# Two score blocks behind each other in differential attention, value products moved behind scores in dilated attention

## Chip, cores and metric

The kernel runs on one core of one Trainium2 chip. The metric is the time of the program in device microseconds. TensorE (PE) does the matrix products, VectorE (DVE) and ScalarE (ACT) read PSUM and work elementwise, GpSimd (POOL) issues some transfers and sums some squares, SyncE (SP) issues the transfers of the weights. A bank is one of the eight PSUM banks of 128 x 512 float32.

## The reference, cut to what matters

The model has two blocks in a row: one layer of gated deltanet with retention and a gated MLP, and then two layers, of which the first mixes with dilated window attention and the second with differential attention, each with an MLP behind it. What is changed lies in the two attention layers of the second block.

```python
def differential_attention(xn, w_qkv, lam, subln_g, w_o, rel_bias, lambda_init):
    q = q.reshape(B, S, B_HEADS, 2, HEAD_DIM_2) * (HEAD_DIM_2 ** -0.5)     # 8 heads, 2 halves of 64
    ...
        logits = jnp.einsum('bqhjd,bkhjd->bhjqk', q_blk, k) + bias[None]
        p = jax.nn.softmax(logits, axis=-1)
        a = p[:, :, 0] - lam_full * p[:, :, 1]
        return jnp.einsum('bhqk,bkhe->bqhe', a, v)
    ...
    o = rms_norm(o, subln_g) * (1.0 - lambda_init)
    return o.reshape(B, S, B_HEADS * 2 * HEAD_DIM_2) @ w_o
```

The sequence has 512 tokens and is cut into 4 blocks of 128 queries; with 8 heads there are 32 blocks of scores, each for two halves j of 64 dimensions against 512 keys. Dilated window attention (16 heads of 64) is softmax(q k + bias) v over windows of keys, in three groups of heads.

## The kernel before

**Layers A and B.** Dilated attention is layer A, differential attention layer B. Each has a projection to queries, keys and values in 12 units of weights; a unit takes 16 steps on PE, a step is one tile and one slice of the contraction: three products of 128 x 128 weights with 512 columns (hi·hi, lo·hi, hi·lo of operands split in two, lines 901 to 903), or for units of values in layer B six of 256 columns (L1413 to L1415). So each layer has 192 steps, numbered 0 to 191. While PE makes the projection it also does the attention of the heads that are there already: tables written out by hand say behind which step each piece comes.

**One block of differential attention.** `block_scores` (L1522) multiplies half j of the queries with half j of the keys: both stand in 64 rows of the array, j = 0 in the upper, j = 1 in the lower, and go to two banks. Three passes (round·round, round·rest, rest·round) make six instructions for a block n. DVE's `scores(n)` (L2932, L2935) reads both banks, adds the bias and takes the maximum. ACT's `exps(n)` (L2306) makes the exponentials, DVE's `difference(n)` (L2942 to L2945) the difference of the two softmaxes. PE turns it with four transposes, `block_turned(n)` (helper at L1005), ACT's `block_taken(n)` (L2315) reads them. `head_values` (L1540) multiplies with the values in four chunks per head, ACT's `head_out` reads the sum, `head_lengths_b` (`brms`, L1499, L1500) sums the squares, `root` (L2249) reads these. `values_kept(u, bank)` (L2279) on ACT reads the two banks of a unit of values.

**Tables.** On PE: B_SCORES, B_TURNED, B_VALUES, B_SUMS. On DVE: B_SCORED (`scores`), B_DIFFS (`difference`), B_REST, B_LOW, B_SPLIT_LO. On ACT: B_EXPS, B_TAKEN, B_OUT, B_ROOTS, B_KEPT, B_SPLIT_HI. A key is a step, its value what is done there. On DVE and ACT the steps only give an order: each engine goes through its own list as fast as its waits let it. After step 191 a tail without a table does blocks 30 and 31 and begins the output projection (`output_b`).

**Banks.** PE asks for a bank with `ring_group`, which waits until the last user of that bank has been read; `BANKS` says which banks a piece may use, and `ring` lists all pieces in PE's order. Projection units use banks 0 and 1, the second unit of a layer banks 2 and 3. All score blocks of layer B use banks 4 and 5, the turned blocks bank 6, the value sums bank 7, `brms` banks 2 and 3.

**Layer A.** A pair of heads n has its scores (L1348, 16 instructions in two row halves, banks 4 and 5), its exponentials, its shares turned (`shares_turned`, 8 transposes, banks 6 and 7) and its value products (`weighted_values`, L1401, 16 instructions of 128 rows and 64 columns, bank 2). ACT's `head_pair` (table A_SUMMED) reads the value products. Within a step PE does scores, then turns, then value products.

Of the kernel before, what the change touches and what calls it, by code (L numbers as in the profile page):

```python
# [203 lines left out]
def build(nc, t, out):  # L204
# [15 lines left out]
    with ctx:  # L220
# [201 lines left out]
        def a_last(n):  # L422
# [11 lines left out]
        A_VALUES = {58: 0, 68: 1, 82: 2, 86: 3, 109: 4, 122: 5, 123: 6, 185: 7, 189: 8}  # L434
# [26 lines left out]
        B_DIFFS = {41: 0, 47: 1, 50: 2, 59: 3, 64: 4, 67: 5, 73: 6, 81: 7, 86: 8, 94: 9, 97: 10, 102: 11, 110: 12, 115: 13,  # L461
                    120: 14, 129: 15, 137: 16, 140: 17, 148: 18, 150: 19, 157: 20, 161: 21, 162: 22, 166: 23, 171: 24, 176: 25,
                    177: 26, 189: 27}
        B_TURNED = {48: 0, 51: 1, 62: 2, 65: 3, 70: 4, 72: 5, 81: 6, 85: 7, 96: 8, 98: 9, 103: 10, 108: 11, 113: 12, 120: 13,
                    125: 14, 132: 15, 139: 16, 145: 17, 152: 18, 154: 19, 163: 20, 167: 21, 169: 22, 179: 23, 186: 24, 189: 25,
                    190: 26}
        B_SCORES = {33: 0, 40: 1, 46: 2, 51: 3, 58: 4, 62: 5, 66: 6, 72: 7, 83: 8, 86: 9, 92: 10, 98: 11, 102: 12, 105: 13,
                    113: 14, 117: 15, 130: 16, 134: 17, 138: 18, 140: 19, 144: 20, 151: 21, 154: 22, 161: 23, 165: 24, 172: 25,
                    177: 26, 180: 27, 188: 28, 189: 29}
        B_VALUES = {67: (0, (0,)), 70: (0, (1,)), 71: (0, (2,)), 73: (0, (3,)), 88: (1, (0,)), 89: (1, (1,)), 90: (1, (2,)),  # L470
                    93: (1, (3,)), 112: (2, (0,)), 117: (2, (1,)), 118: (2, (2,)), 119: (2, (3,)), 133: (3, (0,)),
                    134: (3, (1,)), 136: (3, (2,)), 137: (3, (3,)), 181: (4, (0, 1)), 184: (4, (2, 3)), 188: (5, (0, 1)),
                    189: (5, (2, 3))}
        B_SUMS = {103: 0, 104: 1, 145: 2, 159: 3}
        B_ROOTS = {98: 0, 115: 1, 142: 2, 158: 3}
        B_SCALED = {110: (0,), 129: (1,), 160: (2,), 175: (3,)}
        B_HIGH = {167: (0, 1), 187: (2, 3)}
        B_LOW = {185: (0, 1), 190: (2, 3)}
        B_SCORED = {34: 0, 44: 1, 47: 2, 48: 3, 56: 4, 61: 5, 67: 6, 78: 7, 83: 8, 91: 9, 92: 10, 98: 11, 101: 12, 105: 13,
                    113: 14, 114: 15, 132: 16, 135: 17, 139: 18, 142: 19, 143: 20, 151: 21, 155: 22, 160: 23, 163: 24, 169: 25,  # L480
                    175: 26, 181: 27, 189: 28, 190: 29}
        B_EXPS = {38: 0, 41: 1, 44: 2, 49: 3, 56: 4, 61: 5, 66: 6, 78: 7, 81: 8, 86: 9, 91: 10, 97: 11, 99: 12, 108: 13,
                    112: 14, 120: 15, 131: 16, 132: 17, 136: 18, 145: 19, 150: 20, 153: 21, 159: 22, 161: 23, 166: 24, 169: 25,
                    172: 26, 183: 27, 189: 28, 190: 29}
        B_TAKEN = {42: 0, 51: 1, 57: 2, 59: 3, 66: 4, 69: 5, 80: 6, 83: 7, 89: 8, 95: 9, 103: 10, 107: 11, 114: 12, 121: 13,
                    126: 14, 130: 15, 140: 16, 148: 17, 152: 18, 159: 19, 161: 20, 164: 21, 168: 22, 174: 23, 186: 24, 189: 25,
                    191: 26}
        B_OUT = {72: 0, 88: 1, 123: 2, 133: 3, 175: 4, 191: 5}
        B_SPLIT_HI = {22: 1, 27: 2, 41: 3, 57: 4, 79: 5, 94: 6, 111: 7, 124: 8, 140: 9, 159: 10, 174: 11}
        B_SPLIT_LO = {26: 1, 39: 2, 52: 3, 70: 4, 91: 5, 100: 6, 125: 7, 132: 8, 153: 9, 167: 10, 187: 11}  # L490
        B_ROUND = {17: 0, 23: 1, 25: 2, 38: 3, 54: 4, 64: 5, 71: 6, 79: 7, 105: 8, 115: 9, 123: 10, 131: 11, 139: 12, 148: 13,
                    155: 14, 169: 15}
        B_REST = {21: 0, 27: 1, 28: 2, 39: 3, 62: 4, 71: 5, 75: 6, 82: 7, 107: 8, 116: 9, 123: 10, 133: 11, 143: 12, 156: 13,
                    158: 14, 177: 15}
# [6 lines left out]
        B_KEPT = {40: (2, 0), 47: (2, 1), 88: (5, 0), 95: (5, 1), 167: (10, 0), 173: (10, 1), 183: (11, 0)}  # L501
# [31 lines left out]
        for step in range(A_STEPS):  # L533
            ring += [("s", A_SCORES[step], e) for e in range(2)] if step in A_SCORES else []
            ring += [("pt", A_TURNED[step], e) for e in range(2)] if step in A_TURNED else []
            ring += [("pv", a_last(A_VALUES[step]))] if step in A_VALUES and a_last(A_VALUES[step]) is not None else []
# [7 lines left out]
        for step in range(B_STEPS):  # L544
            ring += [("bs", B_SCORES[step], j) for j in range(2)] if step in B_SCORES else []
            ring += [("at", B_TURNED[step])] if step in B_TURNED else []
            ring += [("bo", B_VALUES[step][0])] if step in B_VALUES and B_VALUES[step][1][-1] == TOK - 1 else []
            ring += [("brms", B_SUMS[step])] if step in B_SUMS else []
        ring += [("at", 27), ("bs", 30, 0), ("bs", 30, 1), ("at", 28), ("bs", 31, 0)]
        ring += [("bs", 31, 1), ("bo", 6), ("at", 29), ("brms", 4), ("brms", 5), ("at", 30), ("at", 31), ("bo", 7)]  # L550
        ring += [("brms", 6), ("brms", 7)]
# [5 lines left out]
                 "bs": (4, 5), "at": (6,), "bo": (7,), ("bo", 7): (5,),  # L557
                 "brms": (2, 3), ("norm", 7): (0,)}
        BANKS.update({("brms", h): (4, 5, 7) for h in range(4, DIFF_HEADS)})
        BANKS.update({("y", 4 * half + c): ((4, 5, 6, 7), (1, 2, 3, 4))[half][c:c + 1] for half in range(2) for c in range(TOK)})  # L560
        BANKS.update({name: tuple(range(8)) for name in MIXER_RING})
# [772 lines left out]
        def attention_a_parts(pe, step):  # L1334

            if step in A_SCORES:
                n = A_SCORES[step]
                tile = A_PAIRS[n][0]
                u, second = A_KEYS[n]
                if second:  # L1340
                    pe.wait_ge(bank_free, p_qkvs[0].g0 + u + 3)
                else:
                    pe.wait_ge(at("a_tile0"), u + 1)
                b = [ring_group(pe, ("s", n, e)) for e in range(2)]
                for k, (i, c) in enumerate(a_parts(n)):
                    for e, (group, _) in enumerate(a_heads(n)):
                        rows = slice(64 * e, 64 * e + 64)
                        ins = nc.tensor.matmul(b[e][:, k * P:(k + 1) * P], a_q[rows, tile, i * P:(i + 1) * P],  # L1348
                                               keys(a_k[rows, tile, :], group, c), start=True, stop=True)
                        if k == TOK - 1:  # L1350
                            ring_filled(ins)
            if step in A_TURNED:
                shares_turned(pe, A_TURNED[step])
            if step in A_VALUES:
                weighted_values(pe, A_VALUES[step])
# [61 lines left out]
        def layer_b_tensor(pe):  # L1417
# [95 lines left out]
        def block_scores(pe, n):  # L1513

            h, i = divmod(n, 4)
            if i == 0:
                pe.wait_ge(at("b_rest"), B_TILES.index((B_KEYS[h], h % 2)) + 1)
            b = [ring_group(pe, ("bs", n, j)) for j in range(2)]
            for k, (q_of, k_of) in enumerate(((b_round, b_round), (b_round, b_rest), (b_rest, b_round))):
                for j in range(2):  # L1520
                    rows = slice(64 * j, 64 * j + 64)
                    ins = nc.tensor.matmul(b[j][:, :], q_of(0, h)[rows, i * P:(i + 1) * P], k_of(1, h)[rows, :],  # L1522
                                           start=k == 0, stop=k == 2)
                    if k == 2:
                        ring_filled(ins)
# [714 lines left out]
        def layer_b_scalar(act):  # L2240
# [628 lines left out]
        def layer_b_vector(dve):  # L2869
# [238 lines left out]
```

## Time and profile before

| | |
|---|---|
| times, three runs | 1914.03, 1914.14, 1915.45 us (median 1914.14) |
| the profiled execution | 1912.97 us, of which the span shown is 1911.1 us |
| granted TensorE clock | 0.999 |
| PE busy | 1897.7 us (99%) |
| DVE, ACT, POOL busy | 1051.3, 808.4, 103.6 us |
| layer A's projection with attention | about 690 to 890 us of the span |
| layer B's projection with attention | about 1289 to 1512 us of the span |

The times of the profile are those of one execution. In the timeline each row is one instruction or several of one line merged (x6): its start, its length, and in a bracket the idle time before it and who ended it. Matrix products are pipelined, so each lasts longer (0.39 us) than the distance to the next start (0.23 us); what a piece costs PE is read from starts, not from lengths.

### The profile page before, as it was taken

How to read it: one execution, taken by the hardware profiler on the slowest of the kernel's cores; microseconds unless marked ns; L12 is line 12 of the kernel's file. 1: busy time of each engine (PE TensorE's matmuls, PEld its weight loads, DVE VectorE, ACT ScalarE, POOL GpSimd, SP SyncE). 2: the span in 40 equal slices, each digit the busy share in tenths (PEclk: the TensorE clock that was granted, in tenths of full speed). 3: DMA queues.
4: the chain of work that ended last, by engine and by line, in shares of the span. 5: the costliest groups of instructions: out<-in, count | busy, mean ns of one | idle time of the engine just before them, and what ended most of it. 6: DMA issues, size and time to landing. Idle time of an engine off the chain costs nothing.

```text
span 1911.1 us, 25491 instructions
## 1 busy us (share of the span) xinstructions
PE 1897.7 (99%) x9523; PEld 1510.6 (79%) x9523; DVE 1051.3 (55%) x1460; ACT 808.4 (42%) x1027; POOL 103.6 (5%) x90
## 2 busy tenths in 40 slices
PE   9999999999999999999999999999999999999998
PEld 7788878888888877777888888887767788888887
DVE  8657765776257667466442244337678644324423
ACT  6382464554134344444432133236666643213312
POOL 0010111000000040000100000010110010000001
PEclk9999999999999999999999999999999999999999
DMA  6223112322322253222223222333322222332231
GB/s 237 88 88 130 33 64 66 110 88 83 113 91 82 80 145 101 68 67 88 89 88 108 90 88 91 107 112 103 105 83 87 67 88 88 102 96 88 88 106 48
DMA packets 146483, 178.91 MB, mean 94 GB/s; under 512 B 3549, under 2 KB 140381, under 8 KB 143968
## 3 DMA queue, kind: packets, MB, share of 16 engines
q1 hardware_dynamic: 143008, 160.44, 25.9%
q0 software_dynamic: 3104, 17.10, 2.8%
q8 instruction: 53, 0.87, 0.2%
q10 hardware_dynamic: 288, 0.26, 0.0%
q14 instruction: 30, 0.25, 0.0%
HBM read 173.48 MB, written 2.20 MB: 92 GB/s over the span
## 4 chain that ended last, share of the span: by engine, by line
PE 96%; DVE 2%; ACT 1%; issue 0%; DMA 0%; SPq 0%; POOL 0%; DVEq 0%; ACTq 0%; POOLq 0%
PE bank L903 28%; PE bank L901 28%; PE bank L902 28%; PE bank L1005 2%; PE bank L1540 2%; PE bank L1522 1%; PE bank L1011 1%; PE bank L1413 1%; PE bank L1415 1%; PE bank L1414 1%; PE bank L1348 1%; PE bank L1401 1%; PE bank L1064 0%; PE bank L1099 0%; DVE w_lo L1631 0%
## 5 line engine op out<-in xcount | busy, mean ns | idle before, releaser
L1625 ACT ACTIVATE w_hi<-raw 128x2048 fp32r<-128x2048 f32 (+2 forms) x151 | 284.0, 1881 | 761.4 <-PE bank L903 756.1
L901 PE MATMUL bank<-n_hi,w_hi 128*128 128x512 f32 x1440 | 577.4, 401 | 2.1 <-DVE w_lo L1631 1.3
L903 PE MATMUL bank<-n_hi,w_lo 128*128 128x512 f32 x1440 | 571.9, 397 | 0.0
L902 PE MATMUL bank<-n_lo,w_hi 128*128 128x512 f32 x1440 | 568.9, 395 | 0.0
L1631 DVE TENSOR_TENSOR w_lo<-raw,w_hi 128x2048 fp32r<-128x2048 f32 (+2 forms) x151 | 340.1, 2252 | 276.6 <-ACT w_hi L1625 275.0
L902 PE MATMUL bank<-ff_lo,w_hi 128*128 128x512 f32 x848 | 334.3, 394 | 0.0
L901 PEld LDWEIGHTS bank<-n_hi,w_hi 128*128 128x128 f32 x1440 | 270.5, 188 | 75.2 <-issue 9.6
L902 PEld LDWEIGHTS bank<-n_lo,w_hi 128*128 128x128 f32 x1440 | 270.7, 188 | 67.5 <-issue 2.9
L903 PEld LDWEIGHTS bank<-n_hi,w_lo 128*128 128x128 f32 x1440 | 270.4, 188 | 63.2
L903 PE MATMUL bank<-ff_hi,w_lo 128*128 128x512 f32 x784 | 312.5, 399 | 0.0
L901 PE MATMUL bank<-ff_hi,w_hi 128*128 128x512 f32 x784 | 307.8, 393 | 0.0
L902 PEld LDWEIGHTS bank<-ff_lo,w_hi 128*128 128x128 f32 x848 | 159.2, 188 | 41.2 <-issue 0.5
L901 PEld LDWEIGHTS bank<-ff_hi,w_hi 128*128 128x128 f32 x784 | 147.1, 188 | 35.5 <-issue 0.3
L903 PEld LDWEIGHTS bank<-ff_hi,w_lo 128*128 128x128 f32 x784 | 147.2, 188 | 34.0
L2687 DVE SCALAR_TENSOR_TENSOR scratch<-bank,rstd 128x512 f32<-128x512 f32 x64 | 44.3, 692 | 149.9 <-PE bank L903 135.6
L2672 DVE TENSOR_TENSOR hT<-hT,bank 128x512 f32<-128x512 f32 (+1 forms) x70 | 48.1, 687 | 135.1 <-PE bank L903 132.2
L2438 DVE SCALAR_TENSOR_TENSOR scratch<-scratch,ffn_w 128x511 f32<-128x511 f32 x88 | 66.1, 751 | 16.8 <-DVE scratch L2438 6.0
L825 POOL TENSOR_TENSOR scratch<-scratch 128x1024 f32<-128x1024 f32 x5 | 13.5, 2709 | 960.5 <-ACT scratch L1756 960.5
L2932 DVE CUSTOM_DVE_ANT_0 scratch<-bank,b_bias 128x512 f32<-128x512 f32 x64 | 44.3, 692 | 28.2 <-PE bank L1522 25.6
L2306 ACT ACTIVATE scratch<-scratch,b_small 128x512 f32<-128x512 f32 x64 | 46.4, 724 | 21.5 <-DVE b_small L2935 19.9
L2426 DVE TENSOR_TENSOR scratch<-bank,rstd 128x512 f32<-128x512 f32 x44 | 30.4, 692 | 32.9 <-PE bank L903 23.2
L2694 DVE TENSOR_TENSOR ff_lo<-scratch,ff_hi 128x1024 f32 x32 | 39.2, 1226 | 8.1 <-ACT ff_hi L2162 7.9
(381 smaller groups left out, 1784.3 us busy)
## 6 DMA issues: line engine op xcount, KB each, us to landing
raw<-in_mlp_w_in SPq DMA_DIRECT2D x32, 1024.0 KB, 5.4
raw<-in_mlp_w_out SPq DMA_DIRECT2D x32, 1024.0 KB, 5.1
raw<-in_w_up SPq DMA_DIRECT2D x22, 1024.0 KB, 5.1
raw<-in_w_units SPq DMA_DIRECT2D x14, 1024.0 KB, 4.8
raw<-in_a_w_qkv SPq DMA_DIRECT2D x12, 1024.0 KB, 5.1
raw<-in_b_w_qkv SPq DMA_DIRECT2D x12, 1024.0 KB, 5.2
b_bias<-bias_table POOLq DMA_DIRECT2D x16, 448.0 KB, 4.4
raw<-in_w_down SPq DMA_DIRECT2D x8, 768.0 KB, 4.5
```

Source lines behind the costliest of these rows:

```text
L901: nc.tensor.matmul(b[:, :], w_hi[:, j % 2, cols], hi, start=start, stop=False)
L902: nc.tensor.matmul(b[:, :], w_hi[:, j % 2, cols], lo, start=False, stop=False)
L903: return nc.tensor.matmul(b[:, :], w_lo[:, j % 2, cols], hi, start=False, stop=final)
L1005: ins = nc.tensor.transpose(b[:, i * P:(i + 1) * P], src(i), ident)
L1625: act.activation(w_hi[:, s, cols], raw[:, s, cols], ACT.Copy).then_inc(hi_ready, 1)
L1631: dve.tensor_tensor(w_lo[:, s, cols], raw[:, s, cols], w_hi[:, s, cols].bitcast(F32), ALU.subtract).then_inc(lo_ready, 1)
L2306: done(act, act.activation(e, e, ACT.Exp, bias=b_small[:, 8 + 2 * (n % 4) + j:9 + 2 * (n % 4) + j], accum_out=b_small[:, 16 + 2 * (n % 4) ...
L2438: ins = dve.scalar_tensor_tensor(y, taken[:, n, 0:SEQ - back], w, y, ALU.mult, ALU.add)
L2672: ins = dve.tensor_tensor(h, h, b[:, :].unsqueeze(1), ALU.add)
L2687: ins = dve.scalar_tensor_tensor(scratch[:, 2 * g + tile, :], b[:, :], 0.0, rstd[:, :], ALU.max, ALU.mult)
L2694: done(dve, dve.tensor_tensor(ff_lo[:, bass.ds(it * 4 + 2 * g, 2), :], scratch[:, 2 * g:2 * g + 2, :], ff_hi[:, bass.ds(it * 4 + 2 * g, 2) ...
L2932: ring_done(dve, dve.tensor_tensor_reduce(b_s[:, n % 4, j, :], b[:, :], reversed_row(b_bias[:, h % 2, j, i * P:i * P + SEQ]), 1.0, -FAR, A ...
```

## The change

In layer B the scores of two blocks, 2m and 2m + 1, are made behind each other (`pair_scores(m)`, table B_PAIRS in place of B_SCORES): block 2m in banks 4 and 5, block 2m + 1 in banks 2 and 3 (the other way round for the last pair). `brms` stays in banks 2 and 3, which it now shares. All tables of layer B are laid out anew, mostly by a few steps; B_SUMS and B_ROOTS move by up to six. The tail does blocks 30 and 31 as one pair in front of the output products. In layer A value products come right behind scores where a step has both (`weighted_values` in front of `shares_turned`), and five of the value products change their step so that six of them share a step with scores (two before). A_SUMMED is not changed.

```diff
-        A_VALUES = {58: 0, 68: 1, 82: 2, 86: 3, 109: 4, 122: 5, 123: 6, 185: 7, 189: 8}
+        A_VALUES = {58: 0, 75: 1, 80: 2, 88: 3, 109: 4, 123: 5, 130: 6, 185: 7, 189: 8}
...
+        B_PAIRS = {37: 0, 47: 1, 58: 2, 67: 3, 82: 4, 91: 5, 102: 6, 113: 7, 130: 8, 137: 9, 143: 10, 152: 11, 167: 12, 176: 13,
+                    187: 14}
...
-        B_SCORES = {33: 0, 40: 1, 46: 2, 51: 3, 58: 4, 62: 5, 66: 6, 72: 7, 83: 8, 86: 9, 92: 10, 98: 11, 102: 12, 105: 13,
-                    113: 14, 117: 15, 130: 16, 134: 17, 138: 18, 140: 19, 144: 20, 151: 21, 154: 22, 161: 23, 165: 24, 172: 25,
-                    177: 26, 180: 27, 188: 28, 189: 29}
...
-        B_SUMS = {103: 0, 104: 1, 145: 2, 159: 3}
-        B_ROOTS = {98: 0, 115: 1, 142: 2, 158: 3}
+        B_SUMS = {108: 0, 111: 1, 150: 2, 165: 3}
+        B_ROOTS = {103: 0, 109: 1, 150: 2, 164: 3}
...
-            ring += [("bs", B_SCORES[step], j) for j in range(2)] if step in B_SCORES else []
+            ring += [("bs", 2 * B_PAIRS[step] + i, j) for i in range(2) for j in range(2)] if step in B_PAIRS else []
...
-                 "bs": (4, 5), "at": (6,), "bo": (7,), ("bo", 7): (5,),
+                 "at": (6,), "bo": (7,), ("bo", 7): (5,),
...
+        BANKS.update({("bs", n, j): (4 + j,) if n % 2 == (n > 29) else (2 + j,) for n in range(B_UNITS) for j in range(2)})
...
+            if step in A_VALUES:
+                weighted_values(pe, A_VALUES[step])
             if step in A_TURNED:
                 shares_turned(pe, A_TURNED[step])
-            if step in A_VALUES:
-                weighted_values(pe, A_VALUES[step])
...
             block_turned(pe, 27)
-            block_scores(pe, 30)
+            pair_scores(pe, 15)
+            block_turned(pe, 28)
             pe.wait_ge(bank_free, ph.g0 + 11 + 3)
             output_b(pe, 0, 0)
+            head_values(pe, 6, (0, 1))
             output_b(pe, 0, 1)
-            block_turned(pe, 28)
-            head_values(pe, 6, (0, 1))
-            block_scores(pe, 31)
             head_values(pe, 6, (2, 3))
             output_b(pe, 0, 2)
+            output_b(pe, 1, 0)
             block_turned(pe, 29)
-            output_b(pe, 1, 0)
...
+        def pair_scores(pe, m):
+
+            h, first = divmod(2 * m, 4)
+            if m == 0:
+                pe.wait_ge(bank_free, p_qkv.g0 + 1 + 3)
+            if first == 0:
                 pe.wait_ge(at("b_rest"), B_TILES.index((B_KEYS[h], h % 2)) + 1)
+            for i in (first, first + 1):
+                b = [ring_group(pe, ("bs", 4 * h + i, j)) for j in range(2)]
+                for k, (q_of, k_of) in enumerate(((b_round, b_round), (b_round, b_rest), (b_rest, b_round))):
+                    for j in range(2):
+                        rows = slice(64 * j, 64 * j + 64)
+                        ins = nc.tensor.matmul(b[j][:, :], q_of(0, h)[rows, i * P:(i + 1) * P], k_of(1, h)[rows, :],
+                                               start=k == 0, stop=k == 2)
+                        if k == 2:
+                            ring_filled(ins)
```

Of the tables that the working speaks of: B_SCORED for blocks 16 to 21 is {132, 135, 139, 142, 143, 149}, B_DIFFS has 16 and 17 at steps 137 and 139, B_TURNED moves block 15 from step 132 to 130 and block 16 from 139 to 142, its value products stay at 133, 134, 136 and 137. ACT's tail does `square(4)` in front of the split of the weights, and `head_out(6)` in front of `block_taken(28)`; DVE's tail does `output_begun_lo` in front of `low(6)`.

## Rows read from the trace of the kernel before

**Rows 1.** The page: span, busy time of each engine, chain that ended last.
```profile
span 1911.1 us, 25491 instructions
...
PE 1897.7 (99%) x9523; PEld 1510.6 (79%) x9523; DVE 1051.3 (55%) x1460; ACT 808.4 (42%) x1027; POOL 103.6 (5%) x90
...
PE 96%; DVE 2%; ACT 1%; issue 0%; DMA 0%; SPq 0%; POOL 0%; DVEq 0%; ACTq 0%; POOLq 0%
```

**Rows 2.** Timeline (start us, length us), PE, around differential block 4 alone.
```profile
1323.61 0.40 PE L902 MATMUL bank<-n_lo,w_hi 128*128 128x512 f32 x1
1323.85 0.39 PE L903 MATMUL bank<-n_hi,w_lo 128*128 128x512 f32 x1
1324.17 0.97 PE L1522 MATMUL bank<-b_parts 64*128 64x512 f32 x6
1325.06 0.50 PE L901 MATMUL bank<-n_hi,w_hi 128*128 128x512 f32 x1
1325.40 0.40 PE L902 MATMUL bank<-n_lo,w_hi 128*128 128x512 f32 x1
```

**Rows 3.** Timeline, PE, dilated attention: scores alone; scores and values; values alone.
```profile
721.76 0.40 PE L903 MATMUL bank<-n_hi,w_lo 128*128 128x512 f32 x1
722.09 1.16 PE L1348 MATMUL bank<-a_k,a_q 64*128 64x128 f32 x16
...
723.51 0.40 PE L902 MATMUL bank<-n_lo,w_hi 128*128 128x512 f32 x1
...
740.33 0.40 PE L903 MATMUL bank<-n_hi,w_lo 128*128 128x512 f32 x1
740.66 1.16 PE L1348 MATMUL bank<-a_k,a_q 64*128 64x128 f32 x16
741.75 1.09 PE L1401 MATMUL bank<-a_pT,consts 128*64 128x128 f32 x16
...
743.12 0.39 PE L902 MATMUL bank<-n_lo,w_hi 128*128 128x512 f32 x1
...
752.66 0.40 PE L903 MATMUL bank<-n_hi,w_lo 128*128 128x512 f32 x1
752.99 1.09 PE L1401 MATMUL bank<-a_pT,consts 128*64 128x128 f32 x16
...
754.35 0.39 PE L902 MATMUL bank<-n_lo,w_hi 128*128 128x512 f32 x1
```

**Rows 4.** Timeline, DVE: reading block 31, then differences of blocks 30 and 31.
```profile
1490.14 0.69 DVE L2932 CUSTOM_DVE_ANT_0 scratch<-bank,b_bias 128x512 f32<-128x512 f32 x1 [1.45 <-PE bank L1522]
...
1491.81 1.42 DVE L861 TENSOR_TENSOR n_lo<-n_behind,b_sq_hi 128x512 fp32r<-128x512 f32 x2
1493.26 0.17 DVE L2942 RECIPROCAL b_small<-b_small 128x2 f32<-128x2 f32 x1
...
1494.83 0.17 DVE L2942 RECIPROCAL b_small<-b_small 128x2 f32<-128x2 f32 x1
```

**Rows 5.** The page, costliest groups: exponentials of a block, two for each.
```profile
L2306 ACT ACTIVATE scratch<-scratch,b_small 128x512 f32<-128x512 f32 x64 | 46.4, 724 | 21.5 <-DVE b_small L2935 19.9
```

**Rows 6.** Timeline, PE: the four chunks of one head's value products.
```profile
1500.96 3.60 PE L1540 MATMUL bank<-consts,b_v 128*128 128x512 f32 x8
1503.99 0.79 PE L901 MATMUL bank<-b_parts,w_hi 128*128 128x512 f32 x1
```

**Rows 7.** Timeline, PE, three places where PE stood; bracket: idle time and releaser.
```profile
1377.23 0.39 PE L903 MATMUL bank<-n_hi,w_lo 128*128 128x512 f32 x1
1377.85 0.47 PE L1499 MATMUL bank<-b_sq_hi,ones_r 128*128 128x512 f32 x1 [0.23 <-POOL b_parts L861]
...
1408.37 0.39 PE L903 MATMUL bank<-n_hi,w_lo 128*128 128x512 f32 x1
1408.89 1.10 PE L1540 MATMUL bank<-consts,b_v 128*128 128x512 f32 x2
...
1483.84 0.50 PE L901 MATMUL bank<-b_parts,w_hi 128*128 128x512 f32 x1 [0.86 <-ACT b_v L2279]
```

More of the change, by code:

```diff
@@ L460, in build @@
         B_UNITS, B_STEPS = 4 * DIFF_HEADS, 12 * 2 * KD
[L461 to L465, printed above, removed]
-                    190: 26}
@@ L467, in build @@
-        B_SCORES = {33: 0, 40: 1, 46: 2, 51: 3, 58: 4, 62: 5, 66: 6, 72: 7, 83: 8, 86: 9, 92: 10, 98: 11, 102: 12, 105: 13,
-                    113: 14, 117: 15, 130: 16, 134: 17, 138: 18, 140: 19, 144: 20, 151: 21, 154: 22, 161: 23, 165: 24, 172: 25,
-                    177: 26, 180: 27, 188: 28, 189: 29}
[L470 to L473, printed above, removed]
@@ L474, in build @@
-        B_SUMS = {103: 0, 104: 1, 145: 2, 159: 3}
-        B_ROOTS = {98: 0, 115: 1, 142: 2, 158: 3}
[L476 to L494, printed above, removed]
+        B_DIFFS = {41: 0, 47: 1, 50: 2, 59: 3, 64: 4, 67: 5, 73: 6, 81: 7, 86: 8, 94: 9, 99: 10, 102: 11, 110: 12, 115: 13,
+                    120: 14, 129: 15, 137: 16, 139: 17, 146: 18, 150: 19, 157: 20, 161: 21, 164: 22, 168: 23, 170: 24, 175: 25,
+                    176: 26, 188: 27}
@@ new lines, in build @@
+        B_TURNED = {48: 0, 51: 1, 62: 2, 65: 3, 70: 4, 72: 5, 81: 6, 85: 7, 95: 8, 97: 9, 102: 10, 108: 11, 113: 12, 120: 13,
+                    125: 14, 130: 15, 142: 16, 146: 17, 151: 18, 152: 19, 161: 20, 167: 21, 169: 22, 178: 23, 185: 24, 188: 25,
+                    189: 26}
+        B_PAIRS = {37: 0, 47: 1, 58: 2, 67: 3, 82: 4, 91: 5, 102: 6, 113: 7, 130: 8, 137: 9, 143: 10, 152: 11, 167: 12, 176: 13,
+                    187: 14}
+        B_VALUES = {67: (0, (0,)), 70: (0, (1,)), 71: (0, (2,)), 73: (0, (3,)), 88: (1, (0,)), 89: (1, (1,)), 90: (1, (2,)),
+                    93: (1, (3,)), 112: (2, (0,)), 117: (2, (1,)), 118: (2, (2,)), 123: (2, (3,)), 133: (3, (0,)),
+                    134: (3, (1,)), 136: (3, (2,)), 137: (3, (3,)), 180: (4, (0, 1)), 183: (4, (2, 3)), 187: (5, (0, 1)),
+                    188: (5, (2, 3))}
@@ new lines, in build @@
+        B_SUMS = {108: 0, 111: 1, 150: 2, 165: 3}
+        B_ROOTS = {103: 0, 109: 1, 150: 2, 164: 3}
+        B_SCALED = {107: (0,), 126: (1,), 164: (2,), 171: (3,)}
+        B_HIGH = {169: (0, 1), 183: (2, 3)}
+        B_LOW = {178: (0, 1), 189: (2, 3)}
+        B_SCORED = {38: 0, 44: 1, 47: 2, 48: 3, 56: 4, 61: 5, 67: 6, 78: 7, 83: 8, 91: 9, 92: 10, 98: 11, 102: 12, 105: 13,
+                    113: 14, 114: 15, 132: 16, 135: 17, 139: 18, 142: 19, 143: 20, 149: 21, 153: 22, 160: 23, 165: 24, 169: 25,
+                    174: 26, 180: 27, 188: 28, 189: 29}
@@ new lines, in build @@
+        B_EXPS = {38: 0, 41: 1, 44: 2, 49: 3, 56: 4, 61: 5, 66: 6, 78: 7, 81: 8, 86: 9, 91: 10, 97: 11, 99: 12, 108: 13,
+                    112: 14, 120: 15, 131: 16, 132: 17, 136: 18, 143: 19, 148: 20, 151: 21, 159: 22, 165: 23, 168: 24, 169: 25,
+                    174: 26, 181: 27, 188: 28, 189: 29}
+        B_TAKEN = {42: 0, 51: 1, 57: 2, 59: 3, 66: 4, 69: 5, 80: 6, 83: 7, 89: 8, 95: 9, 103: 10, 107: 11, 114: 12, 121: 13,
+                    126: 14, 129: 15, 140: 16, 146: 17, 150: 18, 159: 19, 161: 20, 166: 21, 170: 22, 173: 23, 185: 24, 188: 25,
+                    190: 26}
@@ new lines, in build @@
+        B_OUT = {72: 0, 88: 1, 123: 2, 133: 3, 174: 4, 190: 5}
+        B_SPLIT_HI = {22: 1, 27: 2, 47: 3, 57: 4, 79: 5, 94: 6, 111: 7, 124: 8, 140: 9, 159: 10, 173: 11}
+        B_SPLIT_LO = {26: 1, 39: 2, 52: 3, 71: 4, 92: 5, 105: 6, 125: 7, 132: 8, 153: 9, 169: 10, 186: 11}
+        B_ROUND = {19: 0, 23: 1, 24: 2, 38: 3, 54: 4, 64: 5, 71: 6, 79: 7, 105: 8, 115: 9, 119: 10, 131: 11, 139: 12, 146: 13,
+                    153: 14, 169: 15}
+        B_REST = {21: 0, 27: 1, 38: 2, 39: 3, 62: 4, 71: 5, 76: 6, 82: 7, 107: 8, 116: 9, 123: 10, 133: 11, 143: 12, 153: 13,
+                    161: 14, 176: 15}
@@ L495, in build @@
         B_HEADS = (range(0, 4), range(4, 6), range(6, 8))
         B_KEYS = tuple((1, 4, 7, 9)[h // 2] for h in range(DIFF_HEADS))
-        B_KEPT = {40: (2, 0), 47: (2, 1), 88: (5, 0), 95: (5, 1), 167: (10, 0), 173: (10, 1), 183: (11, 0)}
+        B_KEPT = {40: (2, 0), 46: (2, 1), 88: (5, 0), 94: (5, 1), 169: (10, 0), 172: (10, 1), 183: (11, 0)}
         B_VALUE_UNITS = [u for u, (kind, r) in enumerate(UNIT_KINDS[1]) if kind == 2]
@@ L534, in build @@
             ring += [("s", A_SCORES[step], e) for e in range(2)] if step in A_SCORES else []
+            ring += [("pv", a_last(A_VALUES[step]))] if step in A_VALUES and a_last(A_VALUES[step]) is not None else []
             ring += [("pt", A_TURNED[step], e) for e in range(2)] if step in A_TURNED else []
-            ring += [("pv", a_last(A_VALUES[step]))] if step in A_VALUES and a_last(A_VALUES[step]) is not None else []
             ring += [("av",) + A_STAGED[step]] if step in A_STAGED else []
@@ L548, in build @@
             ring += [("brms", B_SUMS[step])] if step in B_SUMS else []
-        ring += [("at", 27), ("bs", 30, 0), ("bs", 30, 1), ("at", 28), ("bs", 31, 0)]
-        ring += [("bs", 31, 1), ("bo", 6), ("at", 29), ("brms", 4), ("brms", 5), ("at", 30), ("at", 31), ("bo", 7)]
-        ring += [("brms", 6), ("brms", 7)]
+        ring += [("at", 27), ("bs", 30, 0), ("bs", 30, 1), ("bs", 31, 0), ("bs", 31, 1), ("at", 28), ("bo", 6)]
+        ring += [("at", 29), ("brms", 4), ("brms", 5), ("at", 30), ("at", 31), ("bo", 7), ("brms", 6), ("brms", 7)]
         ring += norm_ring(6)
@@ L1475, in layer_b_tensor @@
             output_b(pe, 0, 6)
+            output_b(pe, 1, 6)
             output_b(pe, 0, 7)
-            output_b(pe, 1, 6)
             output_b(pe, 1, 7)
@@ L1502, in attention_b_parts @@
         def attention_b_parts(pe, step):
-            if step in B_SCORES:
-                block_scores(pe, B_SCORES[step])
+            if step in B_PAIRS:
+                pair_scores(pe, B_PAIRS[step])
             if step in B_TURNED:
@@ L1511, in attention_b_parts @@
                 head_lengths_b(pe, B_SUMS[step])
-        def block_scores(pe, n):
-            h, i = divmod(n, 4)
-            if i == 0:
-                pe.wait_ge(at("b_rest"), B_TILES.index((B_KEYS[h], h % 2)) + 1)
[L1518 to L1525, printed above, removed]
+        def pair_scores(pe, m):
[3 more added lines that the diff above has]
+            if first == 0:
+                pe.wait_ge(at("b_rest"), B_TILES.index((B_KEYS[h], h % 2)) + 1)
+            for i in (first, first + 1):
[7 more added lines that the diff above has]
+                            ring_filled(ins)
         def block_turned(pe, n):
@@ L2338, in layer_b_scalar @@
             values_kept(11, 1)
+            square(4)
             split_hi(act, ph.u0 + 13, 1)
-            square(4)
             square(5)
             exps(30)
+            head_out(6)
             block_taken(28)
-            head_out(6)
             exps(31)
@@ L2996, in layer_b_vector @@
             head_scaled_b(6)
+            output_begun_lo(dve)
             low(6)
-            output_begun_lo(dve)
             head_scaled_b(7)
```

## The prediction

> **What bounds the kernel now.** I read the page first. PE is busy 1897.7 of 1911.1 us and holds 96% of the chain that ended last [rows 1]; DVE and ACT are busy about half of the span. So a change is worth what it takes from PE's own stream or from PE's waits, and what it gives to DVE and ACT counts only where PE then waits for them. "Busy" hides what matters here, since lengths overlap. I therefore read the timeline of PE by starts, around one piece at a time, and compare with the plain stream, in which an instruction of 512 columns starts 0.24 us behind the last [rows 2]; I take 0.235, so a step of three is 0.70 us and from an L903 over an L901 to the next L902 it is 0.47 us.
>
> **One block alone.** Around block 4, L903 starts at 1323.85, the block at 1324.17 and the first and second product behind it at 1325.06 and 1325.40 [rows 2]. From L903 to the second product that is 1.55 us, where the plain stream has 0.47: the block adds 1.08. Its three passes, each of two instructions that run side by side in the two halves of the rows, are worth 3 x 0.235 = 0.70. The other 0.38 us is paid at the two edges: 0.08 on the way in (0.32 from L903), 0.19 inside (0.89 from the block's start to the next product) and 0.10 behind (0.34 from L901 to L902). I read this as the price of going from 128 rows to two halves of 64 and back.
>
> **Layer B: pairs.** Nothing of the computation goes or comes: 192 instructions of L1522 before and after. 32 blocks are 32 excursions from the stream; in pairs they are 16. If the second block of a pair follows the first at stream rate, it costs 0.70 and not 1.08. 16 x 0.38 = 6.1 us, all on PE. The bounds: nothing, if the 0.38 belongs to each block (its first pass, its banks' waits) and not to the edge; and the 6.1, since more than the excess can't go. I take 6.1, because in layer A a piece behind another of the same kind of short operand saves only a part, but does so across a change of split (next part), and here there is none.
>
> **Layer A: value products behind scores.** Scores alone run from L903 at 721.76 to the second product at 723.51, 1.75 us; values alone from 752.66 to 754.35, 1.69 us; scores with values right behind from 740.33 to 743.12, 2.79 us [rows 3]. Apart they would be 1.75 + 1.69 - 0.47 = 2.97. So a meeting saves 0.18 us. Before there are two (steps 58 and 123), after six: 4 x 0.18 = 0.7 us. That the transposes of steps 80 and 88 now come behind the values changes nothing: they still stand behind a piece with halves. What is moved past what: value product 1 at step 75 frees bank 2 for value product 2 at step 80 only through ACT's `head_pair`, which is behind the exponentials of pair 4; walked as below it is some 0.8 us early, an estimate. Value product 6 goes from 123 to 130 while `A_SUMMED` keeps ACT waiting for it at 123; queued behind it are `exps(7)` and a split of weights that PE needs at step 144. PE takes 14 x 0.70 = 9.8 us to there, the queue about 7; cost nothing.
>
> **Waits that go.** Three places stand out. At 1377.85 `brms` 1 starts 0.62 us behind the last product in place of 0.24, released by POOL: its squares are queued behind a transfer that waits for block 11 [rows 7]. It moves from step 104 to 111: 0.4 gone. At 1408.89 value products of head 3 start 0.52 behind [rows 7]; the turned block 15, which they need, stood one step ahead and will stand three ahead: 0.3 gone. At 1483.84 the first output product waits 0.86 for `values_kept(11, 1)` on ACT [rows 7]; in the new tail three passes more and the transposes of block 28 stand before that wait, 0.70 + 0.4 us, while ACT does the same two things before: 0.9 gone. With the stretched start behind each of the first two, 1.7 us.
>
> **Waits that come.** Banks 2 and 3 are now shared by odd blocks and `brms`, and two blocks lie ready for DVE at once, though it reads them one at a time. A read takes 1.67 us (1490.14 to 1491.81), a difference 1.57 (1493.26 to 1494.83) [rows 4], exponentials on ACT two of 0.72 and their sums, about 1.8 [rows 5]. The closest pairs are at steps 137 and 143. From the first to the second PE spends 1.8 on the pair (0.38 + 6 x 0.235), six steps of 0.70, at least 0.75 on one chunk of values (3.03 us for four) [rows 6] and some 0.4 on a turned block: 7.1 us. DVE needs 1.1 until the first block is there (an estimate: the 0.97 that its six instructions last [rows 2], and a little), 1.67 for block 18, 1.57 for difference 17 that stands between, 1.67 for block 19: 6.0 us. Slack 1.1 us, and block 20 asks for block 18's banks alone, block 21 comes 0.9 later. Walked in the same way, other places are tighter: `brms` 0 at step 108 after block 13 has left bank 2 (0.2 to 0.5), block 15 after `root(1)`, which ACT does behind `exps(12)` (0.3), block 23 after `root(2)` (0.1), block 25's turn in step 188 after `high(3)` on ACT (nothing, or short by 0.3). My walk is good to about half a microsecond at each, so of some six places two or three will cost 0.3 to 0.5: 0.8 us in all, between 0 and 3. The new wait of pair 0 for the second unit's banks costs nothing: DVE leaves them about step 34, PE asks at 37. DMA is unchanged and weights are used 8 us earlier at most over 200 us.
>
> A rule speaks against the change. The Trainium skill, "TensorEngine Tiling (Array Packing)", under "PSUM Bottleneck", says that tiling speeds up TensorE but not the emptying of PSUM, so that the copy may become the bound. By it the second block would gain nothing that DVE doesn't give back; the walk above has the readers done 1.1 us before the banks are asked for, and the sum leaves the rule out but for the 0.8.
>
> **Sum.** 6.1 + 0.7 + 1.7 - 0.8 = 7.7 us. The rows are of an execution of 1912.97 us, with 1.9 around its span of 1911.1; it would take 1905.3, with a span of 1903.4. The median of the three runs is 1914.14, 1.2 above that execution; I take the difference from it: 1906.4 us.
>
> **Rivals.**
> (a) *The edge belongs to the block.* Each block pays its 0.38 because its first pass loads weights in both halves or because a wait precedes it; then pairs save nothing and 0.7 + 1.7 - 0.8 = 1.6 is left: 1912.5. For it: layer A's meeting saved 0.18 and not 0.38 [rows 3]. Against: there the split changes from rows to columns. The skill's same page, under "Key Properties", says that a change of tiling mode drains TensorE and a change of the tile does not; by that the forecast stands and this rival falls, but no row before has two blocks of 64 rows behind each other.
> (b) *Readers late by a little.* If my walk is short by 0.5 us everywhere, PE waits about 0.3 at each of 15 pairs: 4.5 us, 1910.9. For it: PE already waits for ACT and POOL in this stretch [rows 7]. Against: DVE stands idle between reads, 1.45 us before this one [rows 4].
> (c) *Slower.* The same mechanism in force: an odd block is read only after DVE has waited for ACT's exponentials of an earlier block, so read, exponentials, difference and read come one after another (1.67 + 1.8 + 1.57 + 1.67 = 6.7, with the first 1.1 it is 7.8) before banks 2 and 3 are free. Where pairs stand under 7.8 us apart PE waits. It decides from 0.57 us for each of 15 pairs (8.5 us gained in all without waits); at 1.0 each the time is 1914.1 - 8.5 + 15 = 1920.6. Against: only steps 137 to 143 and 143 to 152 are near that distance, others are 8 to 17 us apart.
> (d) *The tail.* The turn of block 28 now stands 2.8 us nearer to its scores. If difference 28 is late, the gain of 0.9 there goes; included in the range.
>
> **Chances.** Forecast 0.77 (own range 1904.5 to 1908.7), (a) 0.08, (b) 0.11, (c) 0.04. A measurement of this kernel tells about 0.2%, 3.8 us, from no change, so the bound is 1910.3. Of (b) two fifths lie below it. Faster 0.81, within 0.2% 0.15, slower 0.04. The range reaches down to 1904.0 (no new wait, and small stalls that I didn't count gone too) and up to 1910.6 (half of (b)); it leaves out (a), (c) and the rest of (b).
>
> **What would show it.** In the profile after, L1522 should come in sixteen groups of 12 that last about 1.6 to 1.7 us from first start to the next other instruction, not 1.8 (2 x 0.89, rival (a)); step distances around a group should show one edge of 0.38. L1348 and L1401 should touch six times. The three waits of [rows 7] should be gone. PE's waits for DVE L2932 (banks not read) or ACT L2249 (`root`) show (b) and (c), above all around steps 108 to 113, 143 to 152 and 188. I would be wrong if the start of block 2m + 1 lies more than 0.3 us behind the last pass of block 2m, or if PE's waits between 1289 and 1512 add up to more than 3 us.

## The result and the profile after

| | before | changed |
|---|---|---|
| median of five runs | 1914.03 us | 1903.89 us |
| lowest and highest | 1913.55, 1915.45 | 1903.48, 1904.47 |
| ratio, 95% interval | | 0.9946 (0.9935 to 0.9957) |
| span of the profiled execution | 1911.1 us | 1902.6 us |
| PE busy | 1897.7 us | 1888.7 us |

The change takes 10.1 us off; 7.7 were forecast, and the time lies 0.1 us under the lower end of the range. The sign and the mechanism were right; one term of the sum, the waits that go, was too small (1.7 us, where 2.8 went).

The page after, in the places of [rows 1]. PE still is the chain; nothing took its place. (Lines of PE's products are one lower than before: L900 to L902; L1523 is the score block, L1004 the transposes.)

```profile
span 1902.6 us, 25492 instructions
...
PE 1888.7 (99%) x9523; PEld 1511.3 (79%) x9523; DVE 1054.4 (55%) x1460; ACT 808.5 (42%) x1027; POOL 101.9 (5%) x90
```

**Where the time went, by stretches.** The two traces have the same 7344 projection products in the same order. So the k-th product of one can be set against the k-th of the other, and the difference of their starts says what was gained up to there:

| stretch | after minus before |
|---|---|
| the first 27 us (input loads, first weights) | +1.0 us |
| from there to layer A | 0.0 |
| layer A | -0.77 |
| MLP between | 0.0 |
| layer B with its output projection | -8.73 |
| the MLP and the end | 0.0 |

The same table for every kernel below gives its layers to some 0.05 us (a layer counted from its first product to its last), where medians scatter by half a microsecond. The first line is no effect of the change: over the ten other profiles told of here it lay between -0.02 and +1.30 us against the profile before, which had one of the quickest starts.

**One pair.** The timeline of PE around blocks 4 and 5 in the changed kernel, which answers to [rows 2]:

```profile
1323.22 0.40 PE L902 MATMUL bank<-n_hi,w_lo 128*128 128x512 f32 x1
1323.55 1.67 PE L1523 MATMUL bank<-b_parts 64*128 64x512 f32 x12
1325.15 0.51 PE L900 MATMUL bank<-n_hi,w_hi 128*128 128x512 f32 x1
1325.49 0.40 PE L901 MATMUL bank<-n_lo,w_hi 128*128 128x512 f32 x1
```

From L902 to the second product behind the pair it is 2.27 us; the plain stream has 0.47, so the pair adds 1.80. Alone the two added 1.08 each. From the pair's start to the next product it is 1.60, as long as one block's 0.89 and three more passes at stream rate.

**Layer A.** Step 80, scores, values and transposes behind each other, which answers to [rows 3]:

```profile
764.42 0.40 PE L902 MATMUL bank<-n_hi,w_lo 128*128 128x512 f32 x1
764.74 1.16 PE L1347 MATMUL bank<-a_k,a_q 64*128 64x128 f32 x16
765.83 1.09 PE L1400 MATMUL bank<-a_pT,consts 128*64 128x128 f32 x16
766.86 1.09 PE L1004 MATMUL bank<-consts,scratch 128*128 128x128 f32 x8
767.71 0.48 PE L900 MATMUL bank<-n_hi,w_hi 128*128 128x512 f32 x1
```

The starts of scores and of values are 1.09 apart as in the meeting of [rows 3].

**Waits of PE between 1289 and 1515.** The view of waits, first of the kernel before, then of the changed one; us in total, times, longest:

```profile
PE bank L901 <- ACT b_v L2279: 0.9, 1, 0.9
PE bank L1499 <- POOL b_parts L861: 0.2, 1, 0.2
```

```profile
PE bank L1523 <- ACT b_stage L2250: 0.3, 1, 0.3
```

This view is short of the truth, and I had leaned on it: it counts only time in which PE had nothing in flight, and lists none that is very short. A wait that is mostly covered by what is in flight hardly shows and still moves the next start. Two such places of the kernel before, which the view does not list:

```profile
1462.67 0.28 PE L1415 MATMUL bank<-w_lo,n_hi 128*128 128x256 f32 x1
1463.06 1.96 PE L1540 MATMUL bank<-consts,b_v 128*128 128x512 f32 x4
...
1513.51 0.39 PE L903 MATMUL bank<-b_parts,w_lo 128*128 128x512 f32 x1
1513.96 0.50 PE L901 MATMUL bank<-b_parts,w_hi 128*128 128x512 f32 x1
```

Products start 0.39 behind a product of 256 columns in place of 0.12, and 0.45 behind one of 512 columns in place of 0.23; with the stretched start behind each, 0.35 and 0.33 us. Read so, the stretch before holds stretched distances at seven places, 2.8 us in all, and the changed one a single place, 0.57 us: block 23, which waited for ACT's `root(2)` to leave bank 2.

```profile
1427.98 0.97 PE L1523 MATMUL bank<-b_parts 64*128 64x512 f32 x6
1429.26 0.96 PE L1523 MATMUL bank<-b_parts 64*128 64x512 f32 x6 [0.31 <-ACT b_stage L2250]
```

The second block of this pair starts 1.28 behind the first in place of 0.80, and the distance from its first pass to the second is 0.33, as at the head of a pair, in place of 0.23; together this is the 0.57. ACT's root in the same kernel's timeline:

```profile
1428.52 0.69 ACT L2250 ACTIVATE b_stage<-bank,consts 128x512 f32<-128x512 f32 x1
```

It ends at 1429.21, and the block starts 0.05 later.

### The profile page after: what moved, and what is told of

It reads as the page before. It is cut to its first block, busy times and chain, and to the rows that moved or that the text cites. A ratio compares the mean times of both kernels' runs of the same rounds, so it can differ in the third digit from the quotient of the medians.

```text
span 1902.6 us, 25492 instructions
## 1 busy us (share of the span) xinstructions
PE 1888.7 (99%) x9523; PEld 1511.3 (79%) x9523; DVE 1054.4 (55%) x1460; ACT 808.5 (42%) x1027; POOL 101.9 (5%) x90
## 4 chain that ended last, share of the span: by engine, by line
PE 95%; DVE 2%; ACT 1%; DMA 1%; SPq 0%; issue 0%; DVEq 0%; ACTq 0%
PE bank L902 28%; PE bank L901 28%; PE bank L900 28%; PE bank L1004 2%; PE bank L1541 1%; PE bank L1523 1%; PE bank L1010 1%; PE bank L1412 1%; PE bank L1413 1%; PE bank L1414 1%; PE bank L1347 1%; PE bank L1400 1%; DMA raw<-in_w_units 1%; PE bank L1063 0%; PE bank L1098 0%; DVE w_lo L1632 0%
## 5 line engine op out<-in xcount | busy, mean ns | idle before, releaser
L900 PE MATMUL bank<-n_hi,w_hi 128*128 128x512 f32 x1440 | 576.2, 400 | 3.2 <-DVE w_lo L1648 1.8
L902 PE MATMUL bank<-n_hi,w_lo 128*128 128x512 f32 x1440 | 571.8, 397 | 0.0
L900 PEld LDWEIGHTS bank<-n_hi,w_hi 128*128 128x128 f32 x1440 | 270.4, 188 | 74.3 <-issue 7.4
L902 PEld LDWEIGHTS bank<-n_hi,w_lo 128*128 128x128 f32 x1440 | 270.3, 188 | 63.2
L902 PE MATMUL bank<-ff_hi,w_lo 128*128 128x512 f32 x784 | 312.5, 399 | 0.0
L900 PE MATMUL bank<-ff_hi,w_hi 128*128 128x512 f32 x784 | 307.8, 393 | 0.0
L900 PEld LDWEIGHTS bank<-ff_hi,w_hi 128*128 128x128 f32 x784 | 147.1, 188 | 35.7 <-issue 0.3
L902 PEld LDWEIGHTS bank<-ff_hi,w_lo 128*128 128x128 f32 x784 | 147.2, 188 | 33.8
```

Of the source, the lines that this page charges most:

```text
L900: nc.tensor.matmul(b[:, :], w_hi[:, j % 2, cols], hi, start=start, stop=False)
L902: return nc.tensor.matmul(b[:, :], w_lo[:, j % 2, cols], hi, start=False, stop=final)
```

## The experiments

Theory: an excursion to half rows or half columns costs PE about 0.38 us at its edges, whatever number of blocks stands inside; and on top of this the new order frees PE of waits. Rivals: the 0.38 belongs to each block; or the waits are the whole gain; or the readers now bound the pairs.

### Layer A alone, layer B alone

The kernel before with the change of A_VALUES and of the order within a step, and the changed kernel with these two undone.

```diff
-        A_VALUES = {58: 0, 68: 1, 82: 2, 86: 3, 109: 4, 122: 5, 123: 6, 185: 7, 189: 8}
+        A_VALUES = {58: 0, 75: 1, 80: 2, 88: 3, 109: 4, 123: 5, 130: 6, 185: 7, 189: 8}
...
+            if step in A_VALUES:
+                weighted_values(pe, A_VALUES[step])
             if step in A_TURNED:
                 shares_turned(pe, A_TURNED[step])
-            if step in A_VALUES:
-                weighted_values(pe, A_VALUES[step])
```

> The kernel before with the change of dilated attention alone (value products behind scores, six meetings for two). My theory: each meeting saves 0.19 us of PE's stream, nothing else moves, so the stretch of layer A gets 0.7 to 0.8 us shorter and the time 1913.3 against 1914.0. Rival: part of what the whole change gained beyond my sum comes from layer A (ACT, which waits longer for value product 6, would then free a later wait): more than 1.5 us.

> The changed kernel with dilated attention as before. My theory: 16 merged excursions of 0.38 us (6.1) and about 3.1 us of PE's waits that went, less 0.6 of one new wait: 8.6 to 8.7 us less than before, 1905.3, all of it between 1289 and 1516 us of the span. Rival: the two layers depend on each other and the sum of both parts is not the whole (10.1 us).

Layer A alone: 1912.93 us against 1913.71 of the kernel before on that chip (ratio 0.9998, 0.9989 to 1.0007: the times alone can't tell it), and by stretches -0.78 in layer A and -0.05 in layer B. Layer B alone: 1905.09 (0.9953, 0.9939 to 0.9967), by stretches -0.01 and -8.73. The parts add up, 0.8 + 8.7 against 9.5, all by stretches; the layers don't touch each other. Value product 6, for which ACT waits seven steps longer, cost nothing.

### Each pair split by one step

```diff
+            ring += [("bs", 2 * B_PAIRS[step], j) for j in range(2)] if step in B_PAIRS else []
+            ring += [("bs", 2 * B_PAIRS[step - 1] + 1, j) for j in range(2)] if step - 1 in B_PAIRS else []
...
             if step in B_PAIRS:
-                pair_scores(pe, B_PAIRS[step])
+                pair_scores(pe, B_PAIRS[step], (0,))
+            if step - 1 in B_PAIRS:
+                pair_scores(pe, B_PAIRS[step - 1], (1,))
```

> The changed kernel, banks, tables and readers the same, but in the steps the second block of each of the 15 pairs comes one step (0.7 us of products) later, so that there are 31 excursions in place of 16. Theory of the edge: each costs 0.38 us again, 15 x 0.38 = 5.7 us more than the changed kernel, 1909.6. Rival (a), the edge belongs to each block and the gain is one of the tables: 0 to 0.5 us more, 1904.

1910.2 us against 1913.71 before on that chip (0.9981, 0.9972 to 0.9990), so 6.3 more than the changed kernel's 1903.9; by stretches layer B has -2.73 for -8.73, 6.0 us back. The timeline of PE shows the two excursions of blocks 4 and 5, each with its edges:

```profile
1324.30 0.39 PE L903 MATMUL bank<-n_hi,w_lo 128*128 128x512 f32 x1
1324.62 0.96 PE L1526 MATMUL bank<-b_parts 64*128 64x512 f32 x6
1325.51 0.50 PE L901 MATMUL bank<-n_hi,w_hi 128*128 128x512 f32 x1
1325.85 0.39 PE L902 MATMUL bank<-n_lo,w_hi 128*128 128x512 f32 x1
1326.08 0.40 PE L903 MATMUL bank<-n_hi,w_lo 128*128 128x512 f32 x1
1326.41 0.96 PE L1526 MATMUL bank<-b_parts 64*128 64x512 f32 x6
1327.30 0.50 PE L901 MATMUL bank<-n_hi,w_hi 128*128 128x512 f32 x1
```

Three products between the halves are enough to pay everything again. The wait of block 23 (0.57) is gone here, and two others came, 0.08 us and 0.59 us at a turned block that found bank 6 not yet read. So 15 edges cost 6.0 + 0.57 - 0.67 = 5.9 us, 0.39 each. Rival (a) is out: banks, tables and readers are those of the changed kernel, only the neighbourhood of the second block is not. What inside an excursion takes the 0.39 us, no run here separates.

### Pairs in two banks

```diff
-        BANKS.update({("bs", n, j): (4 + j,) if n % 2 == (n > 29) else (2 + j,) for n in range(B_UNITS) for j in range(2)})
+        BANKS.update({("bs", n, j): (4 + j,) for n in range(B_UNITS) for j in range(2)})
```

> The changed kernel with all score blocks in banks 4 and 5 again, still in pairs. The second block of a pair must then wait until VectorE has read the first bank of the first: its reading starts 1.1 us behind the start of the block and takes 0.7 a bank, so the second block starts at 1.9 in place of 0.9 and its other half waits to 2.6: 1.0 to 1.7 us for each of 16 pairs, 16 to 27 us more than the changed kernel, 1920 to 1931. Rival: TensorE's queue hides it or the reader is early enough, and two banks do: within 1 us of 1903.9.

1949.65 us (1.0183, 1.0167 to 1.0198), 46 us more than the changed kernel and well above my range. The profiled execution was the slowest of the four, 1955.33, and its layer B alone has 51.4 us more. The waits and one pair:

```profile
PE bank L1523 <- DVE b_small L2933: 29.0, 16, 2.2
```

```profile
1303.64 0.28 PE L1414 MATMUL bank<-w_lo,n_hi 128*128 128x256 f32 x1
1303.85 0.96 PE L1523 MATMUL bank<-b_parts 64*128 64x512 f32 x6
1306.57 0.96 PE L1523 MATMUL bank<-b_parts 64*128 64x512 f32 x6 [1.75 <-DVE b_small L2933]
...
1308.62 0.41 PE L1412 MATMUL bank<-w_hi,n_hi 128*128 128x256 f32 x1
1308.83 0.41 PE L1413 MATMUL bank<-w_hi,n_lo 128*128 128x256 f32 x1
```

The second block starts 2.72 behind the first in place of 0.80: DVE begins to read 1.14 behind the block's start and needs 0.7 and 0.7 for the two banks. I had let PE start again after the first of them, but `pair_scores` asks for both banks before the first product of a block. Sixteen such waits are 31.5 us by starts, above my 16 to 27. What I had left out besides is behind them: at 1308.62 products of 256 columns start 0.21 us apart, where they stood 0.12 apart before the block. The stretch as a whole, by the view of windows (PE, PEld, DVE, ACT, POOL busy; granted clock; DMA share; GB/s):

```profile
1289.00:1569.00 280.00, 251.00 (x1253) 191.59 (x1252) 173.72 (x344) 154.43 (x264) 12.53 (x17) 0.93 0.24 74
```

The granted clock has a mean of 0.93, so PE ran at its lower level, 1.2 GHz, for about a seventh of the stretch; in the changed kernel it is 1.00 there. The 20 us that the waits don't explain are of this size. The four banks are thus what makes pairs pay; with these tables, pairs in two banks are slower than no pairs.

### Four waits taken away without pairs in the steps

```diff
-        B_SUMS = {103: 0, 104: 1, 145: 2, 159: 3}
+        B_SUMS = {103: 0, 111: 1, 145: 2, 159: 3}
```

and in the same way block 15 turned at 130 (and taken at 129), `B_KEPT` (10, 1) at 172 for 173, and the changed kernel's tail on all three engines, with block 30 in banks 2 and 3.

> The kernel before, its 30 score blocks in the steps alone as they were, with four waits of TensorE taken away by moving what they wait for: the sums of head 1 at step 111 for 104, block 15 turned at 130 for 132, the last values of unit 10 kept ahead of the exponentials of block 26, and the changed kernel's tail (which joins blocks 30 and 31). Theory that the waits are a gain of their own beside the pairs: 0.47 + 0.37 + 0.35 us in the steps, and in the tail 0.93 + 0.38 for the joined blocks + 0.3 for a wait at the end of the output projection: 2.8 us less, 1910.9. Rival, that the waits only go because the pairs thin out the work around them: under 1 us less, and the same waits elsewhere.

1911.31 us against 1913.57 on that chip (0.9989, 0.9979 to 0.9998), layer B -2.30. That is 2.3 us where 2.8 were expected; without the 0.38 of the joined blocks 30 and 31 some 2 us of waits are a gain of their own. Three of the four went as priced. The fourth did not: block 15, turned two steps earlier, now waits for ACT's copy of block 14.

```profile
1405.23 0.96 PE L1522 MATMUL bank<-b_parts 64*128 64x512 f32 x6
1406.72 0.63 PE L1005 MATMUL bank<-consts,scratch 128*128 128x128 f32 x4 [0.53 <-ACT consts L2315]
```

The split kernel above has the same wait in the same place, the changed one doesn't: there the pair in front is three passes longer. For this one wait the rival was right, the pair is part of its cure.

### A pair too near

```diff
-        B_PAIRS = {37: 0, 47: 1, 58: 2, 67: 3, 82: 4, 91: 5, 102: 6, 113: 7, 130: 8, 137: 9, 143: 10, 152: 11, 167: 12, 176: 13,
+        B_PAIRS = {37: 0, 47: 1, 58: 2, 67: 3, 82: 4, 91: 5, 102: 6, 113: 7, 130: 8, 137: 9, 139: 10, 152: 11, 167: 12, 176: 13,
```

> The changed kernel with pair 10 at step 139 for 143, so 3.95 us behind pair 9 in place of 7.2. My walk of VectorE in the trace after: block 18 read by 2.7 us, difference 17, block 19's two banks read at 5.1 and 5.8 us from the start of pair 9. Block 21 asks for them at about 4.85: TensorE stands some 1.0 us there, and nothing at any other pair; 0.9 to 1.2 us more in the stretch of layer B than the changed kernel. Rival, that the readers bound the pairs already at 7 us (each pair then waits for VectorE): more than 2 us.

A single execution, 1904.5 us, which alone tells nothing; layer B by stretches -7.55 for -8.73, so 1.18 us more. PE, and DVE's reads of block 19:

```profile
1414.27 0.97 PE L1523 MATMUL bank<-b_parts 64*128 64x512 f32 x6
1416.18 0.96 PE L1523 MATMUL bank<-b_parts 64*128 64x512 f32 x6 [0.94 <-DVE b_small L2933]
```

```profile
1414.60 0.69 DVE L2933 CUSTOM_DVE_ANT_0 scratch<-bank,b_bias 128x512 f32<-128x512 f32 x1
1415.33 0.69 DVE L2933 CUSTOM_DVE_ANT_0 scratch<-bank,b_bias 128x512 f32<-128x512 f32 x1
```

Pair 9 started at 1410.22; block 19 has been read 5.8 us later (1416.02), and block 21 starts 0.16 behind that. Since block 21 would start 0.80 behind block 20, the readers bind at this pair below a distance of 5.2 us (5.96 - 0.80) between pairs. Here it is 4.05, which gives the 1.1 us. The changed kernel keeps 7.3; its two pairs, and DVE's last read of block 19 in it:

```profile
1411.28 1.65 PE L1523 MATMUL bank<-b_parts 64*128 64x512 f32 x12
...
1418.56 1.66 PE L1523 MATMUL bank<-b_parts 64*128 64x512 f32 x12
```

```profile
1416.39 0.69 DVE L2933 CUSTOM_DVE_ANT_0 scratch<-bank,b_bias 128x512 f32<-128x512 f32 x1
```

The read ends at 1417.08, 2.3 us before block 21 asks for its banks at 1419.36. Rivals (b) and (c) are out for the changed kernel, by about 2 us at its closest pair.

### Further in the same direction

```diff
-        B_ROOTS = {103: 0, 109: 1, 150: 2, 164: 3}
+        B_ROOTS = {103: 0, 109: 1, 149: 2, 164: 3}
...
-                if (unit, k) == (0, 1):
-                    weighted_values(pe, 9)
-                elif (unit, k) == (0, 3):
+                if (unit, k) == (0, 3):
+                    weighted_values(pe, 9)
                     weighted_values(pe, 10)
```

with `high(5)` and `low(5)` moved ahead of what waits for these.

> The changed kernel with two more steps of the same kind: ScalarE's root of head 2 ahead of its copy of block 18 (the one wait that came: block 23 stood 0.57 us for it), and in the tail of dilated attention the value products of the last two pairs of heads behind each other. Theory of the edge: 0.57 + 0.38 = 0.95 us less than the changed kernel, 1902.9. Rival, that the second pays with a wait (an output product for the fifth part of the attention): less than 0.6.

> The changed kernel again on the chip of these runs, to set the others beside it: 1903.9, and from its profile the same 8.7 us less in the stretch of layer B and 0.8 in that of layer A; what is above 9.5 us in the difference of the medians is the scatter of the first 27 us (the loads of the input), which differed by 1.0 us between the two profiles.

The changed kernel again: 1903.79 us (0.9950, 0.9936 to 0.9963), by stretches -0.81 and -8.75, its medians 9.8 us apart. The further one: 1903.45 (0.9949, 0.9935 to 0.9962), layer A -1.16 and layer B -8.95, so 0.35 and 0.2 us: under the 0.6 of the rival, though not by its cause. The joined values brought 0.35 of 0.38. The root moved ahead, block 23 came in time, and the next piece waited:

```profile
1426.92 1.66 PE L1522 MATMUL bank<-b_parts 64*128 64x512 f32 x12
1428.95 0.63 PE L1004 MATMUL bank<-consts,scratch 128*128 128x128 f32 x4 [0.37 <-ACT consts L2315]
```

Block 19 is turned right behind the pair and needs bank 6, which ACT, busy with the root, had not left. So one more:

```diff
-130: 15, 142: 16, 146: 17, 151: 18, 152: 19, 161: 20,
+130: 15, 142: 16, 146: 17, 151: 18, 153: 19, 161: 20,
```

> The kernel with the two further steps (value products of the last pairs joined, root of head 2 ahead), and block 19 turned at step 153 for 152, which stood 0.4 us for ScalarE's copy of block 18 there. Theory, that each wait in this stretch is one piece asked for too early by its own amount: the 0.4 us goes, the transposes lose their 0.05 behind a pair, so 0.3 to 0.4 us less than that kernel in the stretch of layer B, 1903.1. Rival, that ScalarE is behind as a whole here and the wait only moves on to the next piece: no change in the stretch.

1903.01 us (0.9943, 0.9930 to 0.9957), layer B -9.31. That is -8.75 and the 0.57 of the one wait, and PE's waits between 1280 and 1515 are an empty list. It is the fastest of all kernels here, by 0.8 us against the changed one (1903.79 on the same chip), a difference that the intervals don't resolve and the stretches do (0.35 in layer A, 0.6 in layer B).

## Why the prediction was right or wrong, point by point

- **What bounds the kernel.** Right: PE, before and after.
- **The price of an excursion, 0.38 us, paid at the edge.** Right. A pair adds 1.80 us where 1.80 was worked out; splitting gave 5.9 us for 15 edges, which for 16 is 6.3 for 6.1.
- **Layer A, 0.7 us.** Right, 0.77 to 0.81 in six profiles.
- **Waits that go, 1.7 us.** This is the step that failed: the mechanism was right, the term was mis-sized; it measured 2.8. The three that I named did go (0.47, 0.37 and 0.93). I had stopped at those that stood out, and left out the rest as small: 0.35 us at values of head 4 (`values_kept(10, 1)` on ACT stood behind the exponentials of block 26), 0.33 at the end of the output projection (a `low` behind a split), 0.19 and 0.15 at turned blocks. The first two alone are 0.7, and their pieces are moved in the diff, so they could have been walked.
- **Waits that come, 0.8 us.** 0.57, a single one, at block 23 behind `root(2)`, the place with the least slack in my walk (0.1 early there, 0.4 late in the trace). The other tight places held. I took "good to half a microsecond" for a cost; most errors fell on the side where they cost nothing.
- **The sum by stretches.** 6.3 + 0.8 + 2.8 - 0.6 = 9.3 where 7.7 was forecast. The stretches give 9.5; the 0.2 between lie in shifts too small to be placed. The medians differ by 10.1 in one measurement and 9.8 in another; what is above 9.5 wasn't settled. It is of the size by which the start of an execution scatters.
- **The range.** Its lower end, 1904.0, allowed 2.4 us for "small stalls that I didn't count" and waits that don't come. The waits took 1.3 of it (1.1 of those that went, 0.2 of those that came), the other terms 0.3, the unplaced shifts 0.2, and the 0.6 between stretches and medians did the rest. The remaining 0.1 is the median before, 1914.14 in the forecast and 1914.03 in the result.
- **Rivals.** (a) is out by the split pairs. (b) and (c) have the mechanism right, as two banks and the near pair show, but their condition isn't met. (c)'s 7.8 us took an exponential into the chain that isn't there: at the closest pair the read of block 19 ended 5.8 us behind the start. (d) didn't happen: in the new tail the first output product starts 0.41 behind the start of the turn of block 28.
- **The rule on emptying PSUM** ("TensorEngine Tiling (Array Packing)", "PSUM Bottleneck", of the Trainium skill) holds for two banks, where PE stood 31.5 us for the reader, and not for four. The other rule of that page, "Key Properties", that a change of mode drains TensorE and a change of tile doesn't, agrees with the 0.39 us an excursion and with nothing lost between the blocks of a pair; that the 0.39 is a drain, no run here shows.

## What to carry to other kernels

Where PE is the bound, read what a small piece costs from starts, from the last product in front to the second behind: pieces in half the rows or columns cost a fixed price for entering and leaving that is worth sharing, if there are banks enough that the second doesn't wait for the reader of the first. List the stretched distances between starts, not the view of waits, since a wait shorter than what is in flight shows no idle time; and give a diff that lays tables out anew credit for every stretched distance whose piece it moves. Set the k-th product of one trace against the k-th of the other: it gives each stretch to 0.05 us where medians scatter by ten times that.

## What the runs showed of the hardware that was not expected

In the kernel with two banks PE stood sixteen times, 1.7 to 2.2 us each, before the second block of a pair, and worked in between. Behind twelve of these stands the granted clock fell to its lower level, 1.2 GHz, for a short stretch, 41 us in all. The first such stretch, by the view of windows (PE, PEld, DVE, ACT, POOL busy; granted clock; DMA share; GB/s):

```profile
1307.85:1311.26 3.41, 3.41 (x18) 3.41 (x18) 3.29 (x4) 0.53 (x2) 0.00 (x0) 0.50 0.10 15
```

Within it products of 256 columns started 0.21 us apart in place of 0.12. Over the 280 us of the stretch the mean is 0.93; the 41 us at half the clock cost 20, beside the 31.5 us of the stands, which makes the 51. Behind the other four (second blocks at 1318.99, 1394.29, 1408.55 and 1428.08) it stayed at 1.00, and what decides is not shown. The four executions had mean clocks of 0.989, 0.992, 0.993 and 0.994 and took 1955.3, 1950.4, 1948.9 and 1947.6 us. Stands of 0.9 us (the near pair, and the tail of the kernel before) showed nothing of the kind: the clock stayed at 1.00.
